# Two post-norm hybrid layers on one core: normalization and latent blocks joined with their neighbours, and weight units fetched and split one phase ahead

## What is computed

```python
h = _layer_norm(h, ln_in_g, ln_in_b)
for l in range(DEPTH):                       # DEPTH = 2
    p = h @ w_in[l]
    p_rwkv, p_mla, p_gate = jnp.split(p, [RWKV_COLS, RWKV_COLS + MLA_COLS], axis=-1)
    y_rwkv = _rwkv7_mix(p_rwkv, ...)         # delta-rule scan, group norm, output gate
    y_mla = _mla(p_mla, ...)                 # rms norms of two latents, up-projections, causal attention
    gate_rwkv, gate_mla = jnp.split(jax.nn.sigmoid(p_gate), N_BRANCHES, axis=-1)
    mixed = gate_rwkv * (y_rwkv @ w_proj_rwkv[l]) + gate_mla * (y_mla @ w_proj_mla[l])
    h = _layer_norm(DEEPNORM_ALPHA * h + mixed @ w_out[l], ln1_g[l], ln1_b[l])
    f = _conv_ffn(h, w_up[l], conv_w[l], conv_b[l], w_down[l])
    h = _layer_norm(DEEPNORM_ALPHA * h + f, ln2_g[l], ln2_b[l])
```

## Time and profile before

| | us |
|---|---|
| median of 3 runs | 4536.91 (4532.87 to 4538.57) |
| the profiled execution | 4534.88 |
| its span, first to last instruction | 4533.1 |
| PE busy | 3877.1 (86% of the span) |
| PE weight loads busy | 3522.9 (78%) |
| DVE, ACT, POOL busy | 2027.8, 1066.1, 936.5 |
| mean granted TensorE clock | 0.932 |

### The profile page before, as it was taken

One profiled execution on the slowest core, in us unless ns is written; L12 is line 12 of the kernel. 1 busy time (PEld: TensorE's weight loads), 2 busy tenths in 40 slices (PEclk: granted clock), 3 DMA queues, 4 the chain that ended last, 5 costly groups with the idle time before them and its releaser, 6 DMA issues. The chain is left out here.

```text
span 4533.1 us, 68171 instructions
## 1 busy us (share of the span) xinstructions
PE 3877.1 (86%) x28391; PEld 3522.9 (78%) x28391; DVE 2027.8 (45%) x2448; ACT 1066.1 (24%) x1504; POOL 936.5 (21%) x464
## 2 busy tenths in 40 slices
PE   3978889898795899999868889898968679999995
PEld 3655888886685899999754569797858579999993
DVE  2145346564415454454422434575633354445454
ACT  3245124222103111121222531341210121212112
POOL 3000320000231333333110014000013133333330
PEclk9988999999898999999978889998988889999997
DMA  4221236421310111111024112553222011111110
GB/s 100 70 68 29 80 110 188 121 70 59 112 32 28 43 47 43 47 47 43 14 63 105 48 34 84 162 163 85 65 98 80 5 47 47 43 47 43 47 38 37
DMA packets 370423, 305.20 MB, mean 67 GB/s; under 512 B 118167, under 2 KB 323571, under 8 KB 370147
## 3 DMA queue, kind: packets, MB, share of 16 engines
q1 hardware_dynamic: 331588, 243.02, 19.0%
q10 hardware_dynamic: 38559, 58.12, 3.7%
HBM read 218.82 MB, written 82.26 MB: 66 GB/s over the span
## 5 line engine op out<-in xcount | busy, mean ns | idle before, releaser
L225 POOL TENSOR_TENSOR w_hi<-w_raw,consts 128x1024 fp32r<-128x1024 f32 (+1 forms) x218 | 392.9, 1802 | 3410.7 <-PE psum L194 1226.1
L194 PE MATMUL psum<-h_hi,w_hi 128*128 128x348 f32 x3792 | 822.7, 326 | 222.1 <-POOL w_lo L227 182.2
L194 PEld LDWEIGHTS psum<-h_hi,w_hi 128*128 128x128 f32 x3792 | 644.9, 190 | 231.3 <-POOL w_lo L227 184.5
L194 PE MATMUL psum<-h_lo,w_hi 128*128 128x348 f32 x3792 | 813.8, 323 | 0.0
L194 PE MATMUL psum<-h_hi,w_lo 128*128 128x348 f32 x3792 | 811.2, 322 | 0.0
L194 PEld LDWEIGHTS psum<-h_lo,w_hi 128*128 128x128 f32 x3792 | 647.4, 190 | 0.0
L194 PEld LDWEIGHTS psum<-h_hi,w_lo 128*128 128x128 f32 x3792 | 642.0, 189 | 0.0
L227 POOL TENSOR_TENSOR w_lo<-w_raw,w_hi 128x1024 fp32r<-128x1024 f32 (+1 forms) x218 | 521.8, 2393 | 17.1
L2314 DVE TENSOR_TENSOR acc<-acc,psum 128x1044 f32<-128x1044 f32 x176 | 217.8, 1238 | 160.2 <-PE psum L194 157.0
L2332 DVE SCALAR_TENSOR_TENSOR cv_g<-up_g,cw,cv_g 128x1044 f32<-128x1044 f32 x44 | 137.7, 3130 | 336.7 <-ACT cv_g L2278 336.7
L2332 DVE SCALAR_TENSOR_TENSOR cv_v<-up_v,cw,cv_v 128x1044 f32<-128x1044 f32 x44 | 146.8, 3336 | 302.3 <-ACT cv_v L2278 302.3
(11 more groups left out here) (260 smaller groups left out, 5276.8 us busy)
## 6 DMA issues: line engine op xcount, KB each, us to landing
w_raw<-in_w_up SPq DMA_DIRECT2D x88, 512.0 KB, 3.8
w_raw<-in_w_in SPq DMA_DIRECT2D x68, 512.0 KB, 5.1
w_raw<-in_w_down SPq DMA_DIRECT2D x44, 512.0 KB, 3.5
gate_scratch<-gst ACTq DMA_DIRECT2D x32, 522.0 KB, 3.0
gbuf<-gate_scratch SPq DMA_DIRECT2D x32, 522.0 KB, 3.6
prep_scratch<-prep ACTq DMA_DIRECT2D x8, 2080.0 KB, 8.2
pc<-prep_scratch SPq DMA_DIRECT2D x20, 832.0 KB, 4.5
rkv_scratch<-mixed_p ACTq DMA_DIRECT2D x24, 522.0 KB, 4.3
```

Source lines behind the costliest of these rows:

```text
L194: last = nc.tensor.matmul(bank[:, n, :], w(k), x(k)[:, nrange(n)], start=(k == 0 and q == 0), stop=(k == kt - 1 and q == 2))
L225: nc.gpsimd.tensor_tensor(w_hi[s][:, 0:width], w_raw[s][:, 0:width], consts[:, 4:5].broadcast_to([P, width]), ALU.mult).then_inc(hi_done.s ...
```

## The change

1. **Weights one phase ahead.** The phases with streamed weights start with units 0 and 1 already split; their own streams begin with unit 2. The units are fetched and split in the phase in front: input normalization (for the first layer's latents), attention (for the RWKV projections), group norm (for the first merge), first merge (for the second), second merge (for the output product), the output product's last units (for the MLP), the MLP's end (for the next layer's latents, the rounding on ACT and the rest on DVE; in the last layer it fetches layer 0's units, which nobody uses).
2. **Latents and up-projections are one phase.** The staging tiles get places of their own, and the up-projections' PSUM halves are swapped, so that the first goes where the mix tile was.
3. **Output product, first layer norm, MLP and second layer norm are one phase.** DVE sums the tiles into `tot` as they are made (one more add per tile), and PE multiplies only that sum by ones. DVE scales block k+1 before it makes `h_lo` of block k. The MLP's first product waits for `h_lo` block by block. `acc` of the MLP is made by ACT from the normalized `acc` (alpha times it plus `ab`), eight instructions after the last `h_hi`; DVE's eight (L2302) go.

Core of the diff:

```diff
+    def split_next(pool, u, hi_done, lo_done, width=1024):
+
+        nc.gpsimd.tensor_tensor(w_hi[u][:, 0:width], w_raw[u][:, 0:width], consts[:, 4:5].broadcast_to([P, width]), ALU.mult).then_inc(hi_done, 1)
+        pool.wait_ge(hi_done, u + 1)
+        nc.gpsimd.tensor_tensor(w_lo[u][:, 0:width], w_raw[u][:, 0:width], w_hi[u][:, 0:width], ALU.subtract).then_inc(lo_done, 1)
+        pool.wait_ge(lo_done, u + 1)
+
...
+                if g == 1:
+                    pool.wait_ge(first_in, 32)
+                    for u in range(2):
+                        pools.did(nc.gpsimd.tensor_tensor(w_hi[u][:, :], w_raw[u][:, :], consts[:, 4:5].broadcast_to([P, 1024]), ALU.mult), f"whi{u}")
+                        pool.wait_ge(pools.sem, pools.of(0, f"whi{u}"))
+                        pools.did(nc.gpsimd.tensor_tensor(w_lo[u][:, :], w_raw[u][:, :], w_hi[u][:, :], ALU.subtract), f"wlo{u}")
...
+                pe.wait_ge(mla_w, 16 * 10)
+                for n, (kind, i) in enumerate(tiles):
+                    if n == 0:
+                        pe.wait_ge(acts.sem, acts.of(0, "gd1"))
+                        pe.wait_ge(dves.sem, dves.of(0, "rb"))
+                    elif n == 1:
+                        pe.wait_ge(acts.sem, acts.of(0, "ln_k"))
+                    elif kind == "kn" and i == 0:
...
+            def _(pool):
+                pool.wait_ge(next_in, 32)
+                for u in range(2):
+                    split_next(pool, u, next_hi, next_lo)
...
+                    for s in range(2):
+                        gate_row(KD // 2 - 1, s)
+                        load_unit(sp, KD + s, s, loaded, split, [(kview(next_kt), w_next[:, :, s * P:(s + 1) * P])])
...
+                    for s in range(2):
+                        split_unit(pool, KD + s, s, KD // 2, loaded, hi_done, split, (used.sem, used.of(KD - 1 + s)), next_kt * P)
+                    pool.wait_ge(split.sem, split.of(KD + 2))
...
+        def norm_pe(pe, n):
+
+            n.pe.did(product32(pset[0], [(ones[:, :], tot[:, :])]), "mean")
+            for k in range(KD):
+                pe.wait_ge(n.act.sem, n.act.of(0, f"sq{k}"))
+                for c in range(NB):
+                    last = nc.tensor.matmul(pset[1][:, c, :], ones[:, :], lsq[k % 2][:, nrange(c)], start=(k == 0), stop=(k == KD - 1))
+                n.pe.did(last, f"v{k}")
+
...
+        def norm_dve(dve, n, other=None):
+            stt = nc.vector.scalar_tensor_tensor
+            dve.wait_ge(n.pe.sem, n.pe.of(0, "mean"))
+            for k in range(KD):
+                n.dve.did(stt(chunks3(acc[:, k, :]), pset[0], -1.0 / DM, chunks3(acc[:, k, :]), ALU.mult, ALU.add), f"c{k}")
+                if other is not None:
+                    other(k)
+            dve.wait_ge(n.act.sem, n.act.of(0, "rs"))
+
+            def scaled(k):
+                n.dve.did(stt(acc[:, k, :], acc[:, k, :], vecs[:, n.g_col + k:n.g_col + k + 1], lrs[:, :], ALU.mult, ALU.mult), f"n{k}")
+            scaled(0)
+            for k in range(KD):
+                if k + 1 < KD:
+                    scaled(k + 1)
+                dve.wait_ge(n.act.sem, n.act.of(0, f"hi{k}"))
+                n.dve.did(stt(h_lo[:, k, :], acc[:, k, :], vecs[:, n.b_col + k:n.b_col + k + 1], h_hi[:, k, :], ALU.add, ALU.subtract), f"lo{k}")
+
...
+                def tile_ready(k):
+                    pe.wait_ge(n1.dve.sem, n1.dve.of(0, f"lo{k}"))
+                with pe.Fori(0, KD // 2) as i:
+                    for s in range(2):
+                        pe.wait_ge(o_split.sem, o_split.of(i * 2 + (s + 1)))
+                        pe.wait_ge(outs.sem, outs.of(i, f"r{s}", 1))
+                        product(pset[s], KD, wtile(w_hi[s], KD), wtile(w_lo[s], KD), hk(m_hi), hk(m_lo)).then_inc(o_used.sem, 1)
+                n1.pe.give(pe)
+                pe.wait_ge(outs.sem, outs.of(KD // 2 - 1, "t1"))
+                norm_pe(pe, n1)
...
+                n1.act.give(act)
+                norm_act(act, n1)
+                nc.scalar.activation(ab[:, :], vecs[:, V_L1B:V_L1B + KD], ACT.Copy, scale=ALPHA).then_inc(ab_done, 1)
+                act.wait_ge(ab_done, 1)
+                for k in range(KD):
+                    act.wait_ge(n1.dve.sem, n1.dve.of(0, f"lo{k}"))
+                    n1.act.did(nc.scalar.activation(acc[:, k, :], acc[:, k, :], ACT.Identity, bias=ab[:, k:k + 1], scale=ALPHA), f"acc{k}")
...
+                        outs.did(nc.vector.tensor_tensor(tot[:, :], tot[:, :], at(acc), ALU.add), f"t{s}")
+                n1.dve.give(dve)
+                norm_dve(dve, n1)
...
+                for s in range(2):
+                    act.wait_ge(next_in[s], 16)
+                    act.wait_ge(pes.sem, pes.of(NP, f"dA{4 * s + 3}"))
+                    nc.scalar.activation(w_hi[s][:, :], w_raw[s][:, :], ACT.Copy).then_inc(next_hi, 1)
+                n2.act.give(act)
+                norm_act(act, n2)
...
+                    dve.wait_ge(dves.sem, dves.of(NP, f"dA{m}"))
+                    if m > 1:
+                        dve.wait_ge(n2.dve.sem, n2.dve.of(0, f"t{m - 1}"))
+                    n2.dve.did(nc.vector.tensor_tensor(tot[:, :], acc[:, 0, :] if m == 1 else tot[:, :], acc[:, m, :], ALU.add), f"t{m}")
+
+                def next_split(k):
+                    if k in (4, 6):
+                        s = (k - 4) // 2
+                        dve.wait_ge(next_hi, s + 1)
+                        nc.vector.tensor_tensor(w_lo[s][:, :], w_raw[s][:, :], w_hi[s][:, :], ALU.subtract).then_inc(next_lo, 1)
+                norm_dve(dve, n2, next_split)
+                dve.wait_ge(next_lo, 2)
```

More of the change, by code:

```diff
@@ L515, in _ @@
                 split.give(sp)
[L516 removed]
+                sp.sem_inc(split.sem, 2)
+                for u in range(2, 5):
                     load_unit(sp, u, u % 2, loaded, split, units[u])
[L518 removed]
+                    if u == 3:
                         sp.dma_start(vecs[:, :], vecs_d[l]).then_inc(vecs_in, 16)
@@ L593, in _ @@
                 rms(6, 2, "k", 0.0)
-                act.wait_ge(mla_w, 16 * nload)
+                assert nload == 10
+                u_acts.give(act)
+                for m, n in enumerate(copied):
+                    act.wait_ge(up_tile, n + 1)
+                    if m >= 2:
+                        act.wait_ge(stored_a[m % 2], 32 * (m // 2))
+                    u_acts.did(nc.scalar.activation(chunks3(st[m % 2][:, :]), pset[(n + 1) % 2], ACT.Copy), f"cp{n}")
+                for c in range(0, NC, 2):
+                    act.wait_ge(up_tile, len(tiles) + c + 1)
+                    if c >= 2:
+                        act.wait_ge(stored_v[0], 16 * (c // 2))
+                    u_acts.did(nc.scalar.activation(vst[0][:, :], psum[0:CH, 6, :], ACT.Copy), f"v{c}")
             @block.vector
@@ L823, in _ @@
                     sp.wait_ge(y_stored[p], 16 * (RT // 2))
+            @block.gpsimd
+            def _(pool):
+                pool.wait_ge(next_in, 32)
+                for u in range(2):
+                    split_next(pool, u, next_hi, next_lo)
             @block.tensor
@@ L1014, in _ @@
                 split.give(sp)
-                for u in range(2):
-                    load_unit(sp, u, u, loaded, split, [(kview(KD), w_in_v[:, :, 3 * RW + u * P:3 * RW + (u + 1) * P])])
+                sp.sem_inc(split.sem, 2)
                 with sp.Fori(0, nt // 2) as i:
@@ L1820, in layer, with _ @@
             w_g_in, bonus_in = sm[3:5]
+            next_in, next_hi, next_lo = sm[5:8]
+            @block.gpsimd
+            def _(pool):
+                pool.wait_ge(next_in, 32)
+                for u in range(2):
+                    split_next(pool, u, next_hi, next_lo, RT * P)
             @block.sync
@@ L2132, in layer, with __init__ @@
         cw = [after(f"cw{i}", [P, 4, 2, FG]) for i in range(2)]
+        tot = after("tot", [P, TP])
+        lrs = tot
+        lsq = [after(f"lsq{i}", [P, TP]) for i in range(2)]
+        ab = after("ab", [P, KD])
         assert cursor[0] <= TOP, (cursor[0], TOP)
+        acc = place("acc", [P, KD, TP], F32, TOP)
+        class Norm:
+            def __init__(self, sems, before, more, g_col, b_col):
+                self.pe = Steps(sems[0], ["mean"] + [f"v{k}" for k in range(KD)])
+                self.act = Steps(sems[1], [f"sq{k}" for k in range(KD)] + ["ln", "rs"] + [f"hi{k}" for k in range(KD)] + more)
+                self.dve = Steps(sems[2], before + [f"c{k}" for k in range(KD)] + ["n0"] + [f"{n}{k + (n == 'n')}" for k in range(KD - 1) for n in ("n", "lo")] + [f"lo{KD - 1}"])
+                self.g_col, self.b_col = g_col, b_col
```

363 lines of the change are left out of this document (166 added, 197 removed).

## The result

| | before | after |
|---|---|---|
| median | 4537.63 (4 runs) | 4344.83 (4342.19 to 4348.69, 4 runs) |
| profiled execution, span | 4534.88, 4533.1 | 4342.19, 4340.4 |
| PE busy | 3877.1 (86%) | 3825.1 (88%) |
| mean granted clock | 0.932 | 0.943 |

The ratio is 0.9581, 95% interval 0.9566 to 0.9595: faster by 193 us. The forecast was 4313, its range 4299 to 4333; the time lies 12 us above the top. The direction was right, and 31 of the 224 us forecast did not come.

A forecast was written before the change was run, and what follows sets the result against it. PE, busy 86%, bounds the kernel, so only its standing time, chiefly waits for `w_lo` and norm chains, can be saved. Terms sum to 223.9 us off 4534.9, 4311.0, forecast 4313 (profiled execution 2.0 under median); range 4299 to 4333.

The forecast's parts named there:

- (g): Output product, first norm, MLP's first product: 51.9 us instead of 94.7, following `h_lo` block by block; 85.6 saved in both layers.
- (a): Input to latents: first product waits for the barrier only, early splits delay the last `h_lo` by 1.5; 11.9 us saved.
- (d): Group norm to first merge: load and split wait goes, splits fall on the centring; 5.5 us twice, 11.0 saved.
- (e): First to second merge: load and split go, small phase opens 1.1 us later; 4.2 twice, 8.4 saved.
- (f): Second merge to output product: splits hide under DVE's last chain but slow two adds; 7.1 us twice, 14.2 saved.
- (c): Attention to RWKV projections: 8.9 us twice, 17.9 saved, less 1 per layer for splits beside attention.
- (b): Latents to up-projections: barrier's 7.75 us go and PE no longer restarts, 2.8; twice, 21.2 saved.
- (h): MLP to second norm and on: 32.7 us saved at the layer turn, 23.0 at the program's end; together 55.7.
- Clock: Rival: PE stays at its lower clock level in the norms and first MLP product; 12 us less, 4325; chance 0.13.
- shared port: Rival: POOL's splits slow DVE's work in (f), attention, input and group norm; some 19 us less, 4332; chance 0.12.
- Units late: Rival: early units come late through queue or slot, so (a), (c) to (f) vanish; 4374; chance 0.03.
- slower: Rival: clock falls in the MLP's first product and stays lower into the MLP's products; 4711; chance 0.01.

The follow-up runs named there:

- runs 5 and 6: Both on the kernel with both starting counts ahead of the norm: 5, norm means over eight blocks again, 4360.87; 6, DVE's old order in both norms, 4352.87.
- the first run: Changed kernel with the MLP phase's starting counts of `pe_steps` and `dve_steps` given ahead of the norm instead of behind it: 4319.15, ratio 0.9527.
- the tenth: On the first run: all five passes of PE's MLP loop written out, the first pass's first two products waiting only for ACT's copies: 4280.89, ratio 0.9450.
- the last: On the tenth: PE's other loops (RWKV projections, both merges, output product) written out too: 4271.75, ratio 0.9422.

## Why the prediction was wrong, point by point

**The step that failed.** The wait of the MLP's first product, in (g): "First `h_lo` done 3.8 after that: 33.5 ... PE follows block by block; a block takes some 1.7 (13.3 / 8) and the last is through at 51 to 52." I took each wait of that product for the one that the diff adds, and did not go through the others that stand on the same instruction. One of them, for `dve_steps`, was met long before in the old kernel, since the norm was another phase; the joining of the phases put its count behind the norm. So PE stood 24.5 us in each layer, until +50.6 instead of +33.5, and the product ended 12.4 us late in layer 1. With the counts moved, the product starts at +33.6, and (g) comes to 58.5 + 13.1 + 13.3 = 84.9 of the 85.6. The sentence "POOL's second unit is held until the centring, where DVE reads PSUM" failed for the same reason: the first unit as well was held until PE had ended the norm. The Trainium skill, GPSIMD Engine Reference, section Specifications, has GpSimd contend with DVE instructions that have two SBUF inputs; the trace agrees: two instructions of L2126, which reads two, took 4.94 beside POOL's last split and 2.52 without it.

**Right in mechanism and size.** (a), (d), (e) to a us. (f) gave 1.0 more. (c) gave 1.9 more, all of it in layer 2 (10.0; layer 1 gave 7.8), where attention in the kernel before was 2.3 us longer than in layer 1, up to its last product; doubling layer 1 could not see that. Within (g) the chain up to the pace of `h_lo`; in the norms the two prices that runs 5 and 6 took apart.

**A little too high.** (b), 19.4 for 21.2: layer 1 gave 11.2, layer 2 only 8.2. The barrier and the unbroken run of PE paid there too (8.03, and 14.20 for the four tiles where it was 16.59). But the latents in front became 2.4 longer: behind the layer loop's turn PE stands once more, four matmuls into the first product, with nothing that releases it,

```profile
2197.82 0.95 PE L196 MATMUL psum<-h_lo,w_hi 128*128 128x348 f32 x2 [1.84 <-issue]
```

which it does not in the kernel before. No term of the prediction has this; it is a pause of the kind described in the last section.

(h), 53.0 for 55.7, is the other term that was a little too high: at the layer's turn 31.6 against 32.7, where the mean took 3.41 instead of 2.6 and the way from the last `h_lo` to the product 4.6 instead of 4.1; at the end 21.4 against 23.0, since the last copy of the output waits 3.38 us for an earlier store where it waited 1.10 before.

**The rivals.** *Clock* (4325) and *shared port* (4332) took in none of this, and the range ended at the second; a product that does not follow block by block was no rival, though the prediction named what would show it ("the MLP's first product in eight pieces 2.5 us apart"). At 12.4 us per layer it would have stood at 4338. *Units late* and *slower* did not occur: no wait for `w_lo` is left in PE's list, and in layer 1 the granted clock is 1.00 in 36 of the 42 windows of 20 us from the first norm's mean on.

**Two slips in the sums**, which change nothing: (a) and (c) to (f) add up to 61.4, not 63.4 (4374 is 4313 plus 61.4), and the price of *shared port* counts again the 2.8 us by which (f) had been lowered already.

## What to carry to other kernels

When two phases are joined, go through every wait of the first instruction behind the seam, not only the new one, and ask for each in which program, and behind what, the count that meets it is given; a starting count belongs at the top. A wait that is met for free in one arrangement can be the last one in the next. And where a fine-grained wait has been put in, look in the trace for its grain: if the pieces do not stand apart, something coarser still holds the whole. Here the hardware loop of the busiest engine was worth writing out whole; written out in part, with the waits as they were, it was slower than the loop (4333.34 against 4319.15).

## What the runs showed of the hardware

The turn of PE's hardware loop is not free, and its price depends on the code around it. In the first run PE stands 0.87 to 1.17 us at three turns of layer 1 (1689.22, 1830.43, 1971.98) with no releaser, in the kernel before 0.67 to 1.01 at four. With one pass written out in front, such turns cost 0.94 to 1.14 there and then 2.00 to 2.30 a few matmuls later, with a stretch at the lower clock level behind. Written out whole, the MLP's products have no pause without a releaser over 0.3 us, and all of PE's loops written out gave 9 us beyond that. The turn of the layer loop is left in all these kernels: PE stands there 1.84 us in the changed kernel, 4.56 in the first run, 3.94 in the tenth and 1.65 in the last.

PE waits for its code in these pauses, as far as a match in time can show it. The traces keep the packets of the instruction queue (`q8 instruction` in the page, 16384 bytes each; in the written-out MLP loop one comes every 17 to 24 us). In the 14 traces, the kernel before among them, PE has 75 pauses of over 0.5 us without a releaser, and every one ends 1.2 to 1.9 us after the end of such a packet; of all of PE's starts in three of these traces only 5% do. In the kernel with the first pass written out packets end at 1663.02 and 1666.19, and PE goes on at 1664.80 and 1667.70. Between the two PE runs three matmuls. A loop that begins just ahead of a packet's end would give this pair, and then the place of the code sets the price and not its length; that is argued, since no run moves the code alone.

The Trainium skill, Runtime: NRT & Kernel Launch, section Instruction fetch mechanics, says that a taken branch whose target is outside the two pages held forces a fetch of the target before execution goes on, and that kernels therefore prefer to be unrolled where possible. The trace agrees: the pauses stand at the turns, each behind a packet, and the loop written out whole is the faster one. That a pass written out in front made the turns dearer (from 0.87 to 1.17 us to a pair of pauses of 3.0 to 3.3 together) is more than the page says.
